# Values from raw x, gates as extra columns, the first conv tap on ScalarE, squares inside products, and key pages over two queues

## What is computed

```python
h = rmsnorm(x, norm_mix[0])              # x * rsqrt(mean(x*x) + eps) * gain
proj = h @ w_in_e[0]                     # columns: conv 1536, z, gates, q, k, v
conv_out = silu(causal_dwconv(buf0, proj[..., :1536], conv_a))   # 4 taps per channel
qa, ka = l2norm(first 512 channels), l2norm(next 512)            # per head of 128
g, beta = f(gate columns); logf = log_sigmoid(gate columns + b_f)
ob = softmax attention over 8 heads of 64, with a bias of summed logf
#   prompt: causal over 1024 tokens
#   sample: eight tokens against 2048 cached keys and values each, 16 pages of 128
oa = gated delta rule(qa, ka, va, g, beta)
```

## Time and profile before

| | us |
|---|---|
| median of three runs | 4102.78 |
| profiled execution, its own time | 4096.77 |
| its span, first to last instruction | 4095.2 |
| TensorE busy | 3694.0 |
| VectorE busy | 1592.4 |
| GpSimd busy | 1302.2 |
| ScalarE busy | 688.5 |

### The profile page before, as it was taken

The page is one execution under the profiler, slowest core; times in us unless marked ns, Lnnn a source line. Parts: engine busy times, 40 slices in busy tenths (PEclk is TensorE's granted clock), DMA queues, the critical chain, the costliest instruction groups (busy, mean ns, idle before and its releaser), DMA issues.

```text
span 4095.2 us, 55933 instructions
## 1 busy us (share of the span) xinstructions
PE 3694.0 (90%) x22605; PEld 3392.7 (83%) x22605; DVE 1592.4 (39%) x1593; ACT 688.5 (17%) x1010; POOL 1302.2 (32%) x727
## 2 busy tenths in 40 slices
PE   5997899799969987899999998966997789999997
PEld 5766666688869876899999998926997689999997
DVE  1015659743243124331222235995305242223142
ACT  1014411122111122110100112103103121101010
POOL 1000013232212321344444444701141234444442
PEclk9899999799769998999999999987999899999998
DMA  1000135644221424111111111140232311111111
GB/s 75 31 21 0 42 109 173 130 130 127 90 96 62 145 72 160 36 47 46 47 46 47 46 46 44 62 104 26 84 118 92 144 36 46 46 47 46 47 47 57
DMA packets 82972, 293.96 MB, mean 72 GB/s; under 512 B 9753, under 2 KB 10026, under 8 KB 79378
## 3 DMA queue, kind: packets, MB, share of 16 engines
q1 hardware_dynamic: 58466, 181.24, 14.5%
q0 software_dynamic: 24368, 110.67, 8.0%
HBM read 265.98 MB, written 26.94 MB: 72 GB/s over the span
## 4 chain that ended last, share of the span: by engine, by line
PE 71%; DVE 11%; issue 10%; ACT 3%; DMA 2%; POOL 2%; DVEq 0%; POOLq 0%; SPq 0%; ACTq 0%
PE ps L525 48%; PE ps L514 3%; PE ps L591 2%; DVE wk L1021 1%; PE ps L1320 1%; PE ps L1626 1%; PE ps L726 1%; PE ps L1313 1%; PE ps L1322 1%; PE ps L1280 1%; PE ps L745 1%; DMA w_raw<-wallb 1%; DVE wk L1023 1%; PE ps L1631 1%; PE ps L1694 1%
## 5 line engine op out<-in xcount | busy, mean ns | idle before, releaser
L293 POOL TENSOR_TENSOR w_hi<-w_raw,ones 128x1024 fp32r<-128x1024 f32 x192 | 466.1, 2427 | 1194.9 <-PE ps L525 1153.9
L525 PE MATMUL ps<-h_hi,w_hi 128*128 128x344 f32 x3072 | 663.5, 325 | 62.1 <-DVE h_lo L487 33.8
L525 PE MATMUL ps<-h_lo,w_hi 128*128 128x344 f32 x3072 | 659.0, 323 | 0.0
L525 PE MATMUL ps<-h_hi,w_lo 128*128 128x344 f32 x3072 | 655.0, 322 | 0.0
L525 PEld LDWEIGHTS ps<-h_hi,w_hi 128*128 128x128 f32 x3072 | 523.5, 191 | 68.4 <-issue 40.6
L294 POOL TENSOR_TENSOR w_lo<-w_raw,w_hi 128x1024 fp32r<-128x1024 f32 x192 | 555.8, 2895 | 15.1
L525 PEld LDWEIGHTS ps<-h_lo,w_hi 128*128 128x128 f32 x3072 | 526.6, 191 | 0.0
L525 PEld LDWEIGHTS ps<-h_hi,w_lo 128*128 128x128 f32 x3072 | 518.4, 190 | 0.0
L514 PE MATMUL ps<-hT,w 128*128 128x344 f32 x1152 | 340.3, 458 | 4.7 <-ACT wk L1081 2.0
L525 PE MATMUL ps<-a_lo,w_hi 128*128 128x344 f32 x1536 | 325.9, 320 | 0.0
L525 PE MATMUL ps<-a_hi,w_hi 128*128 128x344 f32 x1536 | 325.8, 320 | 0.0
(11 more groups left out here) (422 smaller groups left out, 4123.6 us busy)
## 6 DMA issues: line engine op xcount, KB each, us to landing
w_raw<-wallb SPq DMA_DIRECT2D x224, 512.0 KB, 3.5
xT<-kpool POOLq DMA_DIRECT2D x128, 256.0 KB, 3.2
xT<-vpool SPq DMA_DIRECT2D x128, 256.0 KB, 2.9
xT<-cmk POOLq DMA_DIRECT2D x16, 1024.0 KB, 5.4
w<-wall SPq DMA_DIRECT2D x14, 1024.0 KB, 5.1
x<-x_spill SPq DMA_DIRECT2D x32, 270.0 KB, 12.3
x_spill<-xT POOLq DMA_DIRECT2D x2, 4128.0 KB, 19.8
xT<-x_spill POOLq DMA_DIRECT2D x2, 4128.0 KB, 13.9
```

The costliest lines, as they stand in the source:

```text
L293: S["pool"].link(nc.gpsimd.tensor_tensor(w_hi[:, s], w_raw[:, s], one, ALU.mult))
L525: ins = nc.tensor.matmul(ps[:, 3 * (j % 2) + n, 0:N3], wt[:, j % 2, k, :], src[:, k, n * N3:(n + 1) * N3], start=(k == 0 and n_pass == 0), ...
```

## The change

1. Loads: SP loads the vectors, the first half of the value weights, x in four quarters with a semaphore each, then the second half of the value weights into a buffer with 272 columns, of which the last 16 are the gate columns.
2. Values: ScalarE multiplies the gain into the weights; TensorE multiplies raw x. The first six groups are interleaved over the K slices as x arrives; the norm's sums and spread stand between later groups. The gates are the last 16 columns of the second nine groups, and the separate gate products go. VectorE multiplies values and gates by the per-token factor afterwards. The tile of eight sample tokens becomes the last 128 tokens.
3. Conv: ScalarE computes the first tap; the loop is unrolled; the small operations on sample tokens are done once per four chunks; one pair of page scores moves ahead of the first chunk.
4. Squares of the q and k heads: ScalarE makes them in chunks 8 to 11, TensorE sums them inside the last conv groups and the first z groups.
5. Softmax over cached keys: its three TensorE steps stand inside the last two z groups instead of after them.
6. Key pages: SP loads two of every four, GpSimd the other two; SP's weight loads for later pairs are put between its page loads.

```diff
         def sp_loads(sp):
-            for s in range(2):
-                load(0, s)
+            sp.dma_start(vec[:], vecs_in).then_inc(vec_loaded, 16)
+            load(0, 0)
+            for n in range(4):
+                sp.dma_start(xT[:, 2 * n:2 * n + 2], xT_in[:, 2 * n:2 * n + 2]).then_inc(x_loaded[n], 16)
+            sp.dma_start(w_v1[:, :, 0:256], wall[1:2].rearrange("a p (k n) -> p (a k) n", k=KC)).then_inc(w_loaded[1], 16)
+            for dst, src in ((w_v1[:, :, 256:], wgate_in), (pages, pages_in),
+                             (pagec[:], pages_in.rearrange("a (p b) -> (a p) b", b=1))):
+                sp.dma_start(dst, src).then_inc(in_loaded, 16)
+
             for s in range(2):
                 sp.wait_ge(psum_ready, 9 * (s + 1))
                 load(1, s)
...
+                    next_pair(i, s)
+            sp.wait_ge(in_loaded, 48)
+            for n in range(32):
+                sp.wait_ge(fs["free"], n + 1)
+                load_pages(sp, kpool, n // 2, n % 2, "vring", range(2, 4))
+                if n >= 5 and n % 4 == 1 and n <= 25:
+                    next_pair(4 + (n - 5) // 8, (n - 5) // 4 % 2)
             with sp.Fori(0, 16) as r:
...
-        SPREAD_AT = {1: 3584, 6: 3584, 2: 2048, 7: 2048}
+        SPREAD_AT = {0: 2048, 1: 3584, 6: 3584, 2: 2048, 7: 2048}
...
+        def pe_product_with(pe, name, i, src, between):
+
+            p0, g0 = PAIR0[name], GROUP0[name]
+            for s in range(2):
+                pe.wait_ge(w_loaded[s], 16 * (p0 + i + 1))
+                for o in range(2):
+                    j = 2 * s + o
+                    st = (g0 + j) % 2
+                    pe.wait_ge(psum_free, 4 * i + g0 + j - 1)
+                    for k in range(KC):
+                        for n in range(3):
+                            ins = nc.tensor.matmul(ps[:, 3 * st + n, 0:N3], w[:, s, k, o * P:(o + 1) * P],
+                                                   src[:, k, n * N3:(n + 1) * N3], start=(k == 0), stop=(k == KC - 1))
+                        if (j, k) in between and k < KC - 1:
+                            between[j, k](pe)
+                    ins.then_inc(psum_ready, 1)
+                    if (j, KC - 1) in between:
+                        between[j, KC - 1](pe)
...
+        tile_at = [t * P for t in range(QT)] + [T - P]
-        vs = wk[0:NB, 8000:8512]
+        vs = part(wk, 8000, 512)
+        V_BANK = [0, 1, 2, 3, 4, 5] + [(7, 3, 0, 1, 2)[n % 5] for n in range(12)]
...
+            def product(g, k):
+                s, t, at_, n = v_tile(g)
+                return nc.tensor.matmul(ps[:, V_BANK[g], 0:n], xT[:, k, at_:at_ + P], w_v1[:, k, :] if s else w[:, 0, k, :],
+                                        start=(k == 0), stop=(k == KC - 1))
+
+            for k in range(KC):
+                pe.wait_ge(w_scaled, k + 1)
+                pe.wait_ge(x_loaded[k // 2], 16)
+                for g in range(6):
+                    ins = product(g, k)
+                    if k == KC - 1:
+                        ins.then_inc(psum_ready, 1)
+            pe.wait_ge(consts_ready, 1)
+            for g in range(6, 18):
+                if g == 7:
+                    pe_sums(pe, 0, T)
+                elif g == 9:
+                    pe.wait_ge(psum_free, 6)
+                    pe_spread(pe, 0, T)
+                before = max([q for q in range(g) if V_BANK[q] == V_BANK[g]], default=-1)
+                if before >= 0:
+                    pe.wait_ge(psum_free, before + 1)
+                if g >= 9:
+                    pe.wait_ge(w_scaled, 16)
+                for k in range(KC):
+                    ins = product(g, k)
+                ins.then_inc(psum_ready, 1)
+
+        def act_scale_weights(act, s):
+
+            for k in range(KC):
+                wt = w_v1[:, k, :] if s else w[:, 0, k, :]
+                nc.scalar.activation(wt, wt, ACT.Copy, scale=v("norm_mix0", k)).then_inc(w_scaled, 1)
...
+        def act_values(act, g0, g1):
                 act.wait_ge(psum_ready, g + 1)
-                if t < QT:
+                ins = nc.scalar.activation(to[:, s * 256:s * 256 + 256], ps[:, V_BANK[g], 0:256], ACT.Copy)
+                if s:
+                    ins = nc.scalar.activation(ga[0][:, t, :], ps[:, V_BANK[g], 256:272], ACT.Copy)
                 ins.then_inc(psum_free, 1)
+
+        def dve_scale_values(dve):
+
+            dve.wait_ge(psum_free, 18)
+            for t in range(9):
+                x = vf[:, t] if t < QT else vs
+                nc.vector.tensor_scalar(x, x, sm[:, 16 + t:17 + t], None, ALU.mult)
 
         gates_ready, gates_u, gates_exp, gates_done = (sem(n) for n in (
             "gates_ready", "gates_u", "gates_exp", "gates_done"))
         ga = [part(wk, 4200 + 144 * n, 9, 16) for n in range(8)]
...
-            link(vv.tensor_tensor(y, gbank, bias, ALU.add))
+            rows = sm[:, 16:25].rearrange("p (a n) -> p a n", n=1).to_broadcast([P, 9, 16])
+            link(vv.tensor_tensor(y, y, rows, ALU.mult))
+            link(vv.tensor_tensor(y, y, bias, ALU.add))
...
-        def load_pages(eng, src, r, s, done):
-
-            for g in range(4):
+        def load_pages(eng, src, r, s, done, of=range(4)):
+
+            for g in of:
...
-                    load_pages(pool, kpool, r, s, "ring")
+                    load_pages(pool, kpool, r, s, "ring", range(2))
...
-                ins = nc.tensor.transpose(ps[:, 7, c * NB:(c + 1) * NB], vs[:, c * P:(c + 1) * P], ident[0:NB, 0:NB])
+                ins = nc.tensor.matmul(ps[:, 7, c * NB:(c + 1) * NB], vs[:, c * P:(c + 1) * P], ident[:, P - NB:P],
+                                       start=True, stop=True)
...
+        def pe_key_max(pe):
             pe.wait_ge(fs["by_dve"], 1)
...
+        def pe_key_shift(pe):
             pe.wait_ge(fs["by_dve"], 2)
...
+        def pe_key_sum(pe):
             pe.wait_ge(fs["by_dve"], 4)
...
-                dve.wait_ge(fs[f"ring{s}"], i * 256 + 64 * (j + 1))
+                dve.wait_ge(fs[f"ring{s}"], i * 128 + 32 * (j + 1))
+                dve.wait_ge(fs[f"vring{s}"], i * 128 + 32 * (j + 1))
...
+            for c in range(12):
+                st = (g0 + c) % 2
+                act.wait_ge(psum_ready, g0 + c + 1)
+                nc.scalar.activation(c_tail[:, c, :], ps[:, 3 * st + 2, N3 - NB - 3:N3], ACT.Copy)
+                nc.scalar.activation(thirds(c_raw[:, 3:T + 3]), psum_set(st), ACT.Copy).then_inc(psum_free, 1)
+                act.wait_ge(psum_free, g0 + c + 1)
+                nc.scalar.activation(big[:, c, 0:SEQ], c_raw[:, 0:SEQ], ACT.Copy, scale=vec[:, w0 + CA * c:w0 + CA * c + 1])\
+                    .then_inc(conv_tap, 1)
+                if c >= 8:
+                    for h in range(2 * (c - 8), 2 * (c - 8) + 2):
+                        act_qk_square(act, h)
+                act.wait_ge(conv_done, c + c // 4 + 1)
+                nc.scalar.activation(big[:, c, 0:SEQ], big[:, c, 0:SEQ], ACT.Silu).then_inc(conv_silu, 1)
+                if c % 4 == 3:
+                    act.wait_ge(conv_done, c + c // 4 + 2)
+                    nc.scalar.activation(big[:, c - 3:c + 1, SEQ:T], big[:, c - 3:c + 1, SEQ:T], ACT.Silu).then_inc(conv_silu, 1)
+
...
+        def act_qk_square(act, h):
+            if h >= 2:
+                act.wait_ge(l2_ps, h - 1)
+            nc.scalar.activation(qk_sq[:, h % 2, :], big[:, h, :], ACT.Square).then_inc(l2_sq, 1)
...
+        def act_z(act):
+            g0 = GROUP0["z"]
+            for j in range(4):
+                if j == 3:
+                    act_fox_soft(act)
+                act.wait_ge(psum_ready, g0 + j + 1)
+                nc.scalar.activation(thirds(aT[:, j, :]), psum_set((g0 + j) % 2), ACT.Silu).then_inc(psum_free, 1)
...
-                    ins.then_inc(conv_done, 1)
-                    dve_key_scores(dve, i, j, link)
-            for j in range(4):
-                dve_key_scores(dve, 3, j, S["dve"].link)
+            link = S["dve"].link
+            dve_key_scores(dve, 0, 0, link)
+            for c in range(12):
+                i, j = divmod(c, 4)
+                chunk = big[:, c, :]
+                tap = lambda t: vec[:, w0 + CA * c + t:w0 + CA * c + t + 1]
+                dve.wait_ge(conv_tap, c + 1)
+                for t in range(1, CA):
+                    ins = vv.scalar_tensor_tensor(out=chunk[:, 0:SEQ], in0=c_raw[:, t:t + SEQ], scalar=tap(t),
+                                                  in1=chunk[:, 0:SEQ], op0=ALU.mult, op1=ALU.add)
+                    if t < CA - 1:
+                        link(ins)
+                ins.then_inc(conv_done, 1)
+                if j == 3:
+                    dve_conv_rows(dve, i)
+                dve_key_scores(dve, *divmod(c + 1, 4), link)
+            for n in range(13, 16):
+                dve_key_scores(dve, *divmod(n, 4), link)
...
+        def dve_conv_rows(dve, i):
+            for t in range(CA):
+                row = c_st[:, chunks, t, :] if t < 3 else c_tail[:, chunks, 3:]
```

(74 more changed lines are left out.)

115 lines of the change are left out of this document (29 added, 86 removed).

## The result

The changed kernel takes 3998.6 us (median of 4 runs, 3992.3 to 4008.9), the kernel before 4101.9 in the runs beside it: ratio 0.9748, 95% interval 0.9725 to 0.9772. A repeat gave 3999.3 (3985.1 to 4007.4), ratio 0.9758 (0.9731 to 0.9785). The profiled execution took 3992.3 us, span 3990.7. Forecast: 4013, range 3996 to 4041, its own range without rivals 4004 to 4019.

The account below looks back on a forecast made before the run. TensorE held 71% of the chain, VectorE led from conv to delta rule. -63.4 - 25.0 - 1.0 = -89.4 us took 4096.77 to 4007.4; medians sit 6.0 higher: 4013 us, range 3996 to 4041 with rivals, own range 4004 to 4019 (0.57).

Parts of the forecast that it names:

- Values and gates on raw x: Front: first matmul at 9.5 us, values end at 79.8, k product ends at 135.3 instead of 198.67, -63.4 us.
- The rival on a cold front: Values: first 48 matmuls run at 1.2 GHz, 20.7 us more, 4031 us; chance 0.14 together with x's pieces landing late.
- Gates beside k: Front: VectorE's gate work is done by 97 us, covered by k with 38 us to spare, so costs nothing.
- Conv and squares: Conv: TensorE leads at 13.88 us per chunk, five squares add 9.5 us, chunk 11 ends at 178.0.
- the first tap hides nothing: Conv rival: ScalarE's copy, tap and silu hold TensorE as before, 15.6 us per chunk, 20 us less gained, 4033; chance 0.08.
- Pages from two queues: Page scores: a slot's refill takes 6.4 us instead of 8.9, bounds 5.7 and 8.9; scores end at 229.3.
- The slower rival: Page loads: SP's pages land in 27.1 us instead of 3.2, refill 29.6, total 4339 us; chance 0.04.
- Softmax between gate tiles: Before the delta rule: TensorE waits 9 us at the first turn; VectorE's and ScalarE's parts lie under the last z group.
- the -25.0: First conv matmul to delta rule: 253.5 us instead of 278.5.
- First spreads hot: Delta rule's start: first spreads, 3.78 us for 16 records at half speed, run hot; half lies beside VectorE, -1.0 us.
- The rivals that widened the range: Two queues bring nothing (4021 us, 0.17), front starts badly (4022 or 4031, 0.14), first tap hides nothing (4033, 0.08).
- three signs of being wrong: k starts after 95 us; page waits enter conv chunks; the delta rule's shift differs from what the run's end shows.

Follow-up runs that it names:

- Before, started late: The kernel before, with x loaded twice and the first load waited for before anything else is issued; median 4108.4 us.
- Squares in z with the tap on VectorE: The changed kernel with all eight head squares in the first two z groups and the first conv tap back on VectorE; 4002.3 us.
- each half of the change alone: The kernel before with only loads, values and gates changed: 4027.0 us; with only conv, squares, softmax and page loads changed: 4061.7 us.
- one queue: The changed kernel with all four key pages of a score issued by GpSimd again; 3997.1 us, ratio 0.9751.
- the squares here: The changed kernel with all eight head squares moved into the first two z groups; 3987.1 us, ratio 0.9725.

## Why the prediction was right, point by point

*Values and gates on raw x.* First matmul 9.12 (9.5 forecast), k product 79.33 (79.8), its end 134.85 (135.3): -63.8 at the spot where -63.4 was forecast. Sums and spread took 1.90 and 1.91 us in the chain, at full clock, as chosen. The slow start cost about 2.1 us (ten records, 0.43 us apart instead of 0.215) where 2.5 was taken. The rival on a cold front fell: not all 48 matmuls ran at half pace. The Trainium skill (TensorE: Matmul & The Clock Gate, HAM oscillation) says that a product which waits for data between K tiles can start each tile cold. The trace shows no such wait and no such start: only the first ten records were slow, and after them, with six groups per K slice, TensorE was busy 4.00 of 4.00 us while x still arrived.

*Gates beside k.* Nothing waits for them; VectorE's nine scalings begin at 80.0 and the gate sums follow k at once. Right.

*Conv and squares.* Chunk 11's product ends 178.5 us after the first conv matmul (178.0 forecast), scores go on at 186.1 (186.5), end at 229.0 (229.3), turn at 234.3 (234.6), TensorE idle 8.1 (9), silu at 251.5 (252.4), spreads at 252.6 (253.5). The total was right within a microsecond, one reason wrong: the prediction gave VectorE's relief to the first tap and the row operations together. The tap alone was worth nothing in this order. The rival "the first tap hides nothing" had the fact right and the price wrong: 20 us assumed that without it the chunk returns to 15.6, which the row operations had made.

*Pages from two queues.* Refill 6.0 to 6.9 where 6.4 was taken. The page (part 6) gives issue to landing:

```profile
xT<-kpool SPq DMA_DIRECT2D x64, 256.0 KB, 3.1
xT<-kpool POOLq DMA_DIRECT2D x64, 256.0 KB, 3.8
```

A page of GpSimd's lands 0.6 us later than before, and four are issued in the time of two. The Trainium skill (DMA: Bandwidth & Descriptors, Issuing engines are not separate DMA queues) says that a second issuing engine saves only issue time, usually little against the transfer. The trace agrees in kind: two issues fewer on GpSimd are 2.5 us per refill by the 1.23 us each. But it wasn't little here, 9 us at the delta rule, because the refills of the last scores stand in line on the path, and one of them held the 3.42 us pause. The slower rival, SyncE's pages at 27.1 us, fell with the 3.1.

*Softmax between gate tiles.* Counted inside the -25.0 without a price of its own; its price is about nothing. TensorE's 9 us wait, which the prediction named, should have said so.

*First spreads hot.* -2.2 us (89.4 shifted at the spreads, 91.6 at the first product) where -1.0 was taken: half was thought to lie beside VectorE and did not.

*The sum.* -91.6 against -89.4, so 2 us of the miss lie in the steps. The base was 4 us high: the forecast started from a median of three runs, 4102.8, and all 54 runs give 4098.5. Medians fell by 99.2 (4098.5 to 3999.3), so 8 more came behind the first product, in work that the change doesn't touch; the forecast had no term for that. By these 14 us the time fell below the forecast's own range (4004 to 4019) and lies in the wide one only 3 us from its lower end. The rivals that widened the range were all slower, so that its lower end, 8 us below the own range, just held is partly luck. Of the prediction's three signs of being wrong two stayed away (k started at 79.33, and no page wait entered the conv chunks), and the third came: the shift of the delta rule differs from what the end of the run shows, 91.6 against 99.2.

The place that differs most is the delta rule's last rounds, the same distance behind the first product in each kernel (windows as above). Before:

```profile
1057.00:1087.00 30.00, 27.94 (x147) 22.96 (x147) 3.44 (x5) 3.68 (x6) 4.69 (x2) 0.60 0.37 112
1087.00:1117.00 30.00, 28.99 (x168) 24.97 (x168) 4.09 (x9) 4.84 (x10) 0.00 (x0) 0.66 0.13 45
```

Before, started late:

```profile
1068.00:1098.00 30.00, 28.63 (x152) 23.66 (x151) 4.13 (x6) 3.08 (x5) 4.68 (x2) 0.61 0.34 101
1098.00:1128.00 30.00, 28.31 (x162) 24.27 (x162) 3.88 (x8) 5.24 (x11) 0.00 (x0) 0.65 0.17 58
```

Changed:

```profile
965.00:995.00 30.00, 27.94 (x176) 23.84 (x175) 4.12 (x6) 3.68 (x6) 4.69 (x2) 0.74 0.53 157
995.00:1025.00 30.00, 28.30 (x183) 24.07 (x182) 5.74 (x16) 5.44 (x11) 2.51 (x3) 0.75 0.02 10
```

Squares in z with the tap on VectorE:

```profile
958.00:988.00 30.00, 28.54 (x157) 23.55 (x155) 4.13 (x6) 3.13 (x6) 4.91 (x3) 0.63 0.37 103
988.00:1018.00 30.00, 28.72 (x160) 24.73 (x160) 3.58 (x8) 4.79 (x10) 0.00 (x0) 0.63 0.19 60
```

The same work meets a granted clock of 0.60 to 0.66 in three of them and 0.74 to 0.75 in the changed kernel. From the first product to line 1452 in the last round (L1553 in the changed kernel) both run the same 2218 matmul records. Before, then changed:

```profile
826.54:1112.47 285.93, 277.86 (x2218) 243.66 (x2219) 104.50 (x156) 61.01 (x104) 82.44 (x44) 0.92 0.39 118
734.93:1014.82 279.89, 271.81 (x2218) 238.55 (x2219) 104.48 (x156) 61.02 (x104) 82.41 (x44) 0.95 0.42 117
```

The changed kernel did 6.0 us better there, with the higher clock. That the change brings this isn't shown. The last kernel carries all of the front and lost it again (286.82 us, rest 3272.3, above before's 3270.4), and each half of the change alone showed 8 to 10 us that don't add up (9.7 + 7.7 against 7.6). The 8 us lie inside the 21 us by which the same work differs over these kernels (3251.5 to 3272.3). They may still hold a small part that lasts: eight of the nine kernels with some of the change have a rest of 3251.5 to 3265.0, the three with before's code 3264.7 to 3270.4. Why the clock falls at one place and not at another stays open: a common delay doesn't change it, an execution of the same kernel can.

## What to carry to other kernels

Price a change by the shift of a landmark just behind it, which here repeated within 1.3 us; the whole time carried some 20 us of scatter in unchanged work, where the granted clock differs, so one queue, 9 us worse at the delta rule, looked no slower in the median. Where TensorE waits in front of a step, move there what stands ahead of the work that it waits for, as with the squares here (9.3 us), before hiding the step itself. When several edits relieve one engine, undo them one by one: by the rows, batching small operations gave what the moved tap seemed to give, and the tap counts only once TensorE has no slack.

## What the hardware showed unexpectedly

In the delta rule's last rounds TensorE was busy 28 to 29 of 30 us, and its granted clock was still 0.60 to 0.75 on average. In the repeat of the changed kernel a stretch far ahead of it, at 1.00 in the first profile, also fell, with 20.00 of 20 us busy. (Busy time is modelled, so short gaps between matmuls could hide in it.) First profile, then repeat:

```profile
827.00:847.00 20.00, 20.00 (x174) 17.28 (x174) 7.31 (x13) 3.66 (x6) 4.69 (x2) 1.00 0.46 125
```

```profile
827.00:847.00 20.00, 20.00 (x122) 18.22 (x121) 4.56 (x9) 2.87 (x5) 4.71 (x2) 0.66 0.30 90
```

It cost some 10 us there (174 matmul records against 122 in the same time), of which 4.4 are left in the last round (284.3 us from the first product to L1553, against 279.9); a single profile can't tell such a stretch from an effect of the change.
